# A third size of expert in a mixture-of-experts block: up to 32 rows, in four column groups of TensorE

## The reference

```python
group_p = softmax(h @ group_w + group_b);  g = top_1(group_p)          # 4 groups
e_p = softmax((h @ expert_w + expert_b) inside group g)                # 8 experts in a group
top_p, top_i = top_2(e_p)                                              # 2 experts for a token
y[token] = sum over the two of  g_top * top_p * (silu(x @ w_gate[e]) * (x @ w_up[e])) @ w_down[e]
```

```
layer 0: 71 25 68 92 19 32 20 87 27 20 58 43 37 65 71 63 95 41 51 109 89 26 106 41 23 19 20 16 30 51 7 14
layer 1: 56 27 22 31 53 6 38 55 37 68 81 46 40 71 60 17 15 44 8 25 22 23 26 23 19 15 21 13 16 7 18 21
```

## Time and profile before

| what | value |
|---|---|
| median of three executions | 2321.19 us |
| profiled execution, its span | 2321.44 us, 2319.8 us |
| PE, weight loads of PE, DVE, ACT, POOL busy | 81%, 42%, 31%, 19%, 12% of the span |
| HBM read, written | 529.47 MB, 41.78 MB |
| expert weights loaded | 3 x 64 DMAs of 2048 KB |
| stores of expert rows | 51 of 256 KB, 13 of 512 KB |

### The profile page before, as it was taken

One profiled execution on the slowest core, in us unless ns is written; L12 is line 12 of the kernel. 1 busy time (PEld: TensorE's weight loads), 2 busy tenths in 40 slices (PEclk: granted clock), 3 DMA queues, 4 the chain that ended last, 5 costly groups with the idle time before them and its releaser, 6 DMA issues. The chain is left out here.

```text
span 2319.8 us, 23218 instructions
## 1 busy us (share of the span) xinstructions
PE 1889.0 (81%) x7918; PEld 982.4 (42%) x7919; DVE 716.2 (31%) x1243; ACT 429.8 (19%) x748; POOL 279.3 (12%) x355
## 2 busy tenths in 40 slices
PE   2559999889489999999853899999957989987781
PEld 0125444555334444444412546888533334433330
DVE  1130678553411111111227226555331111111114
ACT  2000233311001111111113114444201111111112
POOL 1020254211110000000014010000011000000001
PEclk9779999989689999999985899999968999998896
DMA  9971119210588999999963102000159999999993
GB/s 369 422 261 43 36 60 248 100 58 28 235 339 342 398 409 412 420 386 371 400 260 142 55 0 82 1 1 1 49 219 357 408 411 402 394 402 395 401 414 132
DMA packets 93246, 572.21 MB, mean 247 GB/s; under 512 B 21016, under 2 KB 35096, under 8 KB 61304
## 3 DMA queue, kind: packets, MB, share of 16 engines
q1 hardware_dynamic: 76864, 515.04, 56.7%
q0 software_dynamic: 8832, 30.68, 3.9%
q10 hardware_dynamic: 7480, 25.57, 2.8%
HBM read 529.47 MB, written 41.78 MB: 246 GB/s over the span
## 5 line engine op out<-in xcount | busy, mean ns | idle before, releaser
L1806 PE MATMUL exp_gps<-moew_wg,all_hT 128*64 128x512 f32 (+1 forms) x1024 | 486.1, 615 | 36.8 <-DMA moew_wu<-in_moe_w_up 34.7
L1807 PE MATMUL exp_ups<-moew_wu,all_hT 128*64 128x512 f32 (+1 forms) x1024 | 484.4, 613 | 0.0
L1806 PEld LDWEIGHTS exp_gps<-moew_wg,all_hT 128*64 128x64 f32 (+1 forms) x1024 | 153.4, 153 | 325.9 <-issue 321.0
L1822 PE MATMUL exp_yps<-moew_wd,all_hT 128*64 128x512 f32 (+1 forms) x512 | 243.7, 607 | 39.5 <-issue 39.5
L1824 PE MATMUL exp_yps<-moew_wd,all_hT 128*64 128x512 f32 (+1 forms) x512 | 244.2, 608 | 0.0
L1916 DVE TENSOR_TENSOR all_hT<-all_hT,exp_ups 64x512 f32<-64x512 f32 (+1 forms) x64 | 44.2, 691 | 586.4 <-ACT all_hT L1867 586.4
L1807 PEld LDWEIGHTS exp_ups<-moew_wu,all_hT 128*64 128x64 f32 (+1 forms) x1024 | 154.2, 153 | 50.9 <-issue 50.9
L577 PE MATMUL abp_ps<-abp_w,all_hT 128*128 128x512 f32 x384 | 166.8, 593 | 0.9 <-PE abp_ps L577 0.6
L1925 DVE COPY exp_y<-exp_yps 64x512 f32<-64x512 f32 (+1 forms) x64 | 44.3, 692 | 298.4 <-PE exp_yps L1824 298.4
L1822 PEld LDWEIGHTS exp_yps<-moew_wd,all_hT 128*64 128x64 f32 (+1 forms) x512 | 71.5, 149 | 147.9 <-issue 147.9
L1867 ACT ACTIVATE all_hT<-exp_gps 64x512 f32<-64x512 f32 (+1 forms) x64 | 37.8, 591 | 485.4 <-PE exp_ups L1807 485.4
(11 more groups left out here) (368 smaller groups left out, 2264.3 us busy)
## 6 DMA issues: line engine op xcount, KB each, us to landing
moew_wg<-in_moe_w_gate SPq DMA_DIRECT2D x64, 2048.0 KB, 23.1
moew_wu<-in_moe_w_up SPq DMA_DIRECT2D x64, 2048.0 KB, 29.0
moew_wd<-in_moe_w_down SPq DMA_DIRECT2D x64, 2048.0 KB, 27.7
ada_w<-in_ada_w SPq DMA_DIRECT2D x12, 4096.0 KB, 25.6
ys<-exp_y ACTq DMA_DIRECT2D x51, 256.0 KB, 8.3
abp_w<-in_ab_w_in SPq DMA_DIRECT2D x6, 2048.0 KB, 8.2
ys<-abp_zero SPq DMA_DIRECT2D x32, 256.0 KB
ys<-exp_y ACTq DMA_DIRECT2D x13, 512.0 KB, 10.1
```

The costliest lines, as they stand in the source:

```text
L1806: nc.tensor.matmul(gps[0:rows, :], x[:, k, 0:rows], w.g[q][:, k, :], start=(k == 0), stop=(k == KD - 1))
L1807: last = nc.tensor.matmul(ups[at:at + rows, :], x[:, k, 0:rows], w.u[q][:, k, :], start=(k == 0), stop=(k == KD - 1))
L1822: nc.tensor.matmul(yps[0][0:rows, :], hT[:, k, 0:rows], w.d[q][:, k, 0:512], start=(k == 0), stop=(k == HT_N - 1))
```

## The change

A third path, Q = 32, is added beside 128 and 64, on all engines.

- PE computes gate and up of a small expert in four column groups: the left and right halves (256 columns) of the gate matrix on PSUM partitions 0 to 31 and 32 to 63, those of the up matrix on 64 to 95 and 96 to 127. So the hidden rows come out as 64 partitions of 256 values, and two transposes take the place of four. The down product has four groups of 256 columns too.
- For that split of the hidden dimension all sizes now take the down matrix in pairs of rows: partition p holds rows 2p, 2p+1 and 256+2p, 256+2p+1, in place of 4p to 4p+3. A partition's 16 KB come from two places of 8 KB each.
- ACT and DVE work on 256 columns for such an expert; each copies its half of the output in two pieces of 32 x 256.
- 32 rows are gathered and 32 stored for it. The zero fill covers rows 32 to 127.

```diff
-                lo = 0 if b >= E else P // 2
+                lo = 0 if b >= E else P // 4
...
 def load_down(sp, a, layer, w, e, q):
-    src = a["moe_w_down"][layer].rearrange("e (p k) n -> e p (k n)", p=P)[bass.ds(e, 1)]
-    sp.dma_start(w.d[q][:].rearrange("p k n -> p (k n)"), src.rearrange("o p m -> (o p) m")).then_inc(w.d_ready[q], 16)
+    src = a["moe_w_down"][layer].rearrange("e (k p two) n -> e p k (two n)", p=P, two=2)[bass.ds(e, 1)]
+    sp.dma_start(w.d[q][:].rearrange("p (k two) n -> p k (two n)", two=2),
+                 src.rearrange("o p k n -> (o p) k n")).then_inc(w.d_ready[q], 16)
...
+        def sized(eng, rows, work):
             with eng.If(rows > H):
                 work(P)
             with eng.Else():
-                work(H)
+                with eng.If(rows > Q):
+                    work(H)
+                with eng.Else():
+                    work(Q)
...
                 def up(rows):
+                    if rows == Q:
+                        for k in range(KD):
+                            for bank, wt, lo in ((gps, w.g[q], 0), (ups, w.u[q], H)):
+                                for j in range(2):
+                                    last = nc.tensor.matmul(bank[lo + j * Q:lo + (j + 1) * Q, 0:HC], x[:, k, 0:Q],
+                                                            wt[:, k, j * HC:(j + 1) * HC],
+                                                            start=(k == 0), stop=(k == KD - 1))
+                        last.then_inc(gu_used, 1)
+                        return
...
                 def down(rows):
+                    if rows == Q:
+                        for k in range(2):
+                            last = nc.tensor.transpose(hps[:, k, 0:H], h_by[H:P, 0, k, :], c.ident[H:P, H:P])
...
+                    if rows == Q:
+                        for k in range(HT_N):
+                            for j in range(4):
+                                last = nc.tensor.matmul(yps[j // 2][j * Q:(j + 1) * Q, 0:HC], hT[:, k, 0:Q],
+                                                        w.d[q][:, k, j * HC:(j + 1) * HC],
+                                                        start=(k == 0), stop=(k == HT_N - 1))
+                        last.then_inc(d_used, 1)
+                        return
```

More of the change, by code:

```diff
@@ L1699, in experts @@
         LOOPS = (E - 1) // S
-        H = P // 2
+        H, Q = P // 2, P // 4
+        HC = HID // 2
         idx = [s.sb(f"idx{i}", [P, 1], I32) for i in range(S)]
@@ L1711, in experts @@
         x_by = [x.rearrange("r (p k) -> r k p", k=KD) for x in xg]
-        h_by = h.rearrange("r (p k) -> r k p", k=HT_N)
+        h_by = h.rearrange("r (k p two) -> r k two p", p=P, two=2)
         xps = [s.ps(f"xps{i}", [P, 4, P]) for i in range(2)]
@@ L1736, in by_rows @@
             rows = eng.value_load(r.cnt[0:1, bass.ds(n, 1)], min_val=0, max_val=TOK)
+            sized(eng, rows, work)
+        def sized(eng, rows, work):
             with eng.If(rows > H):
@@ L1812, in down @@
                     at = 0 if rows == P else H
-                    for k in range(HT_N):
-                        last = nc.tensor.transpose(hps[:, k, 0:rows], h_by[at:at + rows, k, :],
-                                                   c.ident[at:at + rows, at:at + rows])
+                    if rows == Q:
+                        for k in range(2):
+                            last = nc.tensor.transpose(hps[:, k, 0:H], h_by[H:P, 0, k, :], c.ident[H:P, H:P])
+                    else:
+                        for k in range(HT_N):
+                            last = nc.tensor.transpose(hps[:, k, 0:rows], h_by[at:at + rows, k // 2, k % 2, :],
+                                                       c.ident[at:at + rows, at:at + rows])
                     last.then_inc(htr, 1)
@@ L1828, in turn @@
                 rows = pe.value_load(r.cnt[0:1, bass.ds(n, 1)], min_val=0, max_val=TOK)
[L1829 to L1832, removed]
+                sized(pe, rows, up)
                 if more:
@@ L1836, in turn @@
                 pe.wait_ge(ht_done, n + 1)
[L1837 to L1840, removed]
+                sized(pe, rows, down)
             x_transposes(0, 0, 0)
@@ L1866, in silu @@
                     act.wait_ge(h_done, n + 1)
+                    if rows == Q:
+                        nc.scalar.activation(sg[H:P, 0:HC], gps[0:H, 0:HC], ACT.Silu).then_inc(sg_done, 1)
+                        return
                     nc.scalar.activation(sg[at:at + rows, :], gps[0:rows, :], ACT.Silu).then_inc(sg_done, 1)
@@ L1871, in rows_out @@
                     act.wait_ge(y_free[q], i * 16 + 16)
-                    nc.scalar.copy(y[q][0:rows, 0:512], yps[0][0:rows, :]).then_inc(y_act, 1)
+                    if rows == Q:
+                        nc.scalar.copy(y[q][0:Q, 0:HC], yps[0][0:Q, 0:HC])
+                        nc.scalar.copy(y[q][0:Q, HC:2 * HC], yps[0][Q:2 * Q, 0:HC]).then_inc(y_act, 1)
+                    else:
+                        nc.scalar.copy(y[q][0:rows, 0:512], yps[0][0:rows, :]).then_inc(y_act, 1)
                     act.wait_ge(y_act, n + 2)
@@ L1875, in rows_out @@
                     act.dma_start(ys[bass.ds(n, 1), 0:rows].rearrange("o p n -> (o p) n"), y[q][0:rows, :]).then_inc(y_free[q], 16)
[L1877 to L1880, removed]
+                sized(act, rows, silu)
                 if more:
                     x_copy(n + 1, (q + 1) % S)
[L1883 to L1886, removed]
+                sized(act, rows, rows_out)
             x_copy(0, 0)
@@ L1915, in hidden @@
                     dve.wait_ge(sg_done, n + 1)
+                    if rows == Q:
+                        nc.vector.tensor_tensor(h[H:P, 0:HC], sg[H:P, 0:HC], ups[H:P, 0:HC], ALU.mult).then_inc(h_done, 1)
+                        return
                     nc.vector.tensor_tensor(h[at:at + rows, :], sg[at:at + rows, :], ups[at:at + rows, :],
@@ L1921, in rows_out @@
                     dve.wait_ge(htr, n + 1)
-                    nc.vector.tensor_copy(hT[:, :, 0:rows], hps[:, :, 0:rows]).then_inc(ht_done, 1)
+                    if rows == Q:
+                        nc.vector.tensor_copy(hT.rearrange("p (a b) r -> p b a r", b=2)[:, :, :, 0:Q],
+                                              hps[:, 0:2, 0:H].rearrange("p b (a r) -> p b a r", a=2)).then_inc(ht_done, 1)
+                    else:
+                        nc.vector.tensor_copy(hT[:, :, 0:rows], hps[:, :, 0:rows]).then_inc(ht_done, 1)
                     dve.wait_ge(d_used, n + 1)
                     dve.wait_ge(y_free[q], i * 16 + 16)
+                    if rows == Q:
+                        nc.vector.tensor_copy(y[q][0:Q, 2 * HC:3 * HC], yps[1][H:H + Q, 0:HC])
+                        nc.vector.tensor_copy(y[q][0:Q, 3 * HC:4 * HC], yps[1][H + Q:P, 0:HC]).then_inc(y_dve, 1)
+                        return
                     nc.vector.tensor_copy(y[q][0:rows, 512:1024], yps[1][at:at + rows, :]).then_inc(y_dve, 1)
[L1927 to L1930, removed]
+                sized(dve, rows, hidden)
                 if more:
                     x_copy(n + 1, (q + 1) % S)
[L1933 to L1936, removed]
+                sized(dve, rows, rows_out)
             x_copy(0, 0)
```

## The result

Four executions of the changed kernel took 2261.4 to 2274.2 us, median 2267.23 us. The kernel before, beside it on the same chip, took 2320.82 us. The ratio is 0.977 (95% interval 0.974 to 0.979): 2.3% faster. The forecast was 2271.3 us.

What follows compares the result with a forecast made beforehand. DMA bounds layer 1, DMA and PE within 3% layer 0; traffic, idle time and ends less down-matrix cost save 24.0 and 26.1 us, together 50.1 from 2321.4: 2271.3 us. Own range 2250 to 2295 us, 8 in 10 2248 to 2303.

Steps and rivals of the forecast that it cites:

- PE: Small experts' matmuls: four column groups run side by side, step 0.215 us for 0.43, turn 8.6 us for 13.76.
- Rival A: Small experts' matmuls: four groups bring PE nothing, layer 0 keeps its end, 2299 us; chance 0.07.
- Traffic of a small expert: Gather and store of 32 rows: 1.18 us saved an expert (0.62 to 1.73), gather loss taken by row.
- Rival B: Expert DMA: small gather loses as much as a 64-row one, 8 KB pieces cost as 4 KB; 2303 us, chance 0.11.
- What counts is traffic: Expert layers: faster PE alone is worth nothing in layer 1, at most DMA's idle 2% in layer 0.
- Idle DMA in layer 0: Layer 0 expert stretch: of 11 us idle DMA, 5 us gained (0 to 11) as gaps behind small experts close.
- Ends: Last small expert behind each layer's last weights: 3.5 us saved a layer (1 to 7), depending on PE's clock.
- Down matrix: Down weight loads in 8 KB pieces: 1 us cost a layer, bounds 0 and 7.3 us.
- Zero fill: Projection block: 4.2 MB more zeros, some 17 us, hidden by PE; cost 0, at worst about 5 us.
- Rival C: Expert loop: PE's longer loop must refetch instructions, up to 27 us a round, about 2640 us; chance 0.05.
- q8 packets inside the expert loops: Sign in the profile after: instruction-queue packets there would show PE's loop being fetched anew and the forecast wrong.
- What would show it: Profile signs: PE waits for layer 0 weights from about its fifth expert, expert stretches about 518 and 493 us.

Runs made afterwards that it cites:

- PE alone: Changed kernel with small experts gathering and storing 64 rows and the old zero fill, against the kernel before: 2304.5 us, ratio 0.992.
- traffic alone: Kernel before with 32 rows gathered and stored for small experts and the larger zero fill, computing still on 64 rows: 2297.2 us, ratio 0.989.
- the second trace: Changed kernel, unaltered, profiled once more in a later comparison with the kernel before: profiled execution 2259.6 us, median 2265.7 us, ratio 0.976.

## Why the prediction was right, point by point

- **PE.** The step was taken as 0.215 us, measured 0.22. The turn was forecast at 8.6 us, measured 8.25. Rival A is refuted. Behind an idle stretch it can start at half clock, as in the earlier trace rows. The last small expert of layer 0, kernel after (start us, duration us):

```profile
1159.23 0.64 PE L1818 MATMUL exp_gps<-moew_wg,all_hT 128*32 128x256 f32 x2 [6.15 <-DMA moew_wu<-in_moe_w_up]
...
1159.66 0.64 PE L1818 MATMUL exp_gps<-moew_wg,all_hT 128*32 128x256 f32 x2
...
1164.65 0.38 PE L1818 MATMUL exp_gps<-moew_wg,all_hT 128*32 128x256 f32 x2
...
1164.87 0.38 PE L1818 MATMUL exp_gps<-moew_wg,all_hT 128*32 128x256 f32 x2
```

  Behind 6.15 us of idle time the granted clock is 0.50 (1159.2 to 1164.2 us) and steps are 0.43 us apart, as forecast; from 1164.7 us it is 1.00 and they are 0.22 us apart.
- **Traffic of a small expert.** 1.18 us forecast for each. DMA work fell by 16 and 22 us: 1.1 us for each of 14 and 20. The 32-row gather was taken at 0.87 us, in the middle of 0.31 and 1.42. With the forecast's own 1.23 and 1.73 us for the larger gathers the runs bracket it: 0.49 under a 128-row one (1.23 - 0.49 = 0.74), 0.75 under a 64-row one (1.73 - 0.75 = 0.98). A 64-row gather was taken to cost 0.5 us more than a 128-row one, measured as (551.8 - 538.2) / 29 = 0.47. That is near a loss by row (0.87) and far from bytes alone (0.31) and from a fixed loss for each gather (1.42). Rival B is refuted in both its halves, by these runs and by the down matrix alone. Stretches with a 32-row gather, kernel after (last column GB/s), against the earlier trace rows:

```profile
1934.50:1936.90 2.40, 2.40 (x6) 1.12 (x7) 0.69 (x1) 0.58 (x1) 0.00 (x0) 1.00 1.02 335
...
2004.90:2006.70 1.80, 0.00 (x0) 0.00 (x0) 0.63 (x1) 0.49 (x1) 0.00 (x0) 1.00 1.02 314
...
2101.00:2103.00 2.00, 0.00 (x0) 0.00 (x0) 0.00 (x0) 1.28 (x1) 0.00 (x0) 1.00 1.02 303
```

  About half as long as the 4.8 us of a 64-row one, at the same lower rate: sixteen such stretches read 283 to 359 GB/s. This is what the Trainium skill's "SBUF — State Buffer", Door 1: The DMA port swizzle, leads one to expect, that 0 to 31 and 0 to 63 reach the same half of the ports; the traces agree in the rate and in 128 rows going without loss. They do not show the ports themselves, and no run gathered 64 rows into other partitions, so the number of partitions and their place are not told apart.
- **What counts is traffic.** Half right. In layer 1 it is all that counts: 19.8 us from traffic, 3.2 from PE. In layer 0 the sentence that a faster PE alone is worth "at most the idle 2% of DMA" gave 11 us with the ends aside, and PE alone brought 15.4, of which the end is some 3, while traffic alone brought 2.9 of the 13 by which the DMA work fell. There traffic counts only once PE is faster. The sum came out right because both were changed at once.
- **Idle DMA in layer 0.** 5 us forecast. DMA's idle time there went from 29 to 21 us (17 in the second trace); without the layer's end (11 us, then 8 and 5, next point) 18 to 13 and 12 us: 5 to 7.
- **Ends.** From the last weight packet to the last matmul it was 11.0 and 10.8 us before, 7.9 and 8.0 after, 5.4 and 4.8 in the second trace. Saved 3 and 6 us a layer; 3.5 was forecast between 1 and 7. Which of the two comes is a matter of the clock, and by luck the two traces show one each. The last down product of layer 0 in the first and in the second trace of the kernel after (busy us, mean ns):

```profile
L1846 PE MATMUL exp_yps<-moew_wd,all_hT 128*32 128x256 f32 x32 | 3.6, 628 | 0.4 <-issue 0.4
```

```profile
L1846 PE MATMUL exp_yps<-moew_wd,all_hT 128*32 128x256 f32 x32 | 1.9, 381 | 0.4 <-issue 0.4
```

  Same code, at a granted clock of 0.53 (1167.9 to 1171.5 us) and of 1.00 (1161.6 to 1163.5 us in the second trace). This is some of the scatter of the kernel after, and the range had 5 us either way for the ends.
- **Down matrix.** 1 us a layer, measured none.
- **Zero fill.** Forecast to be hidden, which held: the projection block ended at 437.2 us against 436.4. Its size was off. The stores started 0.8 us later and ended at about 412 us, against 408: some 4 us longer, not 17. The 17 were worked out at the rate of stores from 64 partitions, and stores from 96 ran faster (last section). SP's waits at the block's end, kernel after, against the earlier trace rows:

```profile
SPq L72 <- PEq L72: 24.1, 1, 24.1
SPq L72 <- DMA ys<-abp_zero: 5.6, 1, 5.6
```

- **Rival C.** Refuted as a cost of every round. Queues that carried packets from 710 to 1145 us, kernel after:

```profile
q1 hardware_dynamic: 14302, 160.24, 90.4%
q10 hardware_dynamic: 2384, 8.00, 4.6%
q0 software_dynamic: 2128, 7.08, 4.5%
```

  No instruction queue, with 1260 matmul and load instructions in a round. But the prediction had named q8 packets inside the expert loops as a sign of this rival, and there are some: 9 from 1700 to 2272 us, where the kernel before has 5, most of them in the layer's first round and at its end. PE in the gate/up products of the first two small experts of layer 1, kernel after:

```profile
1743.06 0.40 PE L1818 MATMUL exp_gps<-moew_wg,all_hT 128*32 128x256 f32 x1
1745.70 0.41 PE L1818 MATMUL exp_gps<-moew_wg,all_hT 128*32 128x256 f32 x2 [2.24 <-issue]
...
1759.57 0.64 PE L1818 MATMUL exp_gps<-moew_wg,all_hT 128*32 128x256 f32 x2 [3.39 <-issue]
```

  Both gaps lie between two steps of one product, which have nothing to wait for, and a q8 packet lies near the start of each (1743.2 and 1756.9 us; the gaps start at 1743.5 and 1756.2). The second trace has the same two gaps, 2.5 and 3.1 us, with a packet at each. So most likely the new path was fetched there at its first use, and PE stood still for 2 to 3 us, less than the 4.5 us that the rival took. It happens once and not in each round, and in a layer that DMA bounds, where no cost in time is seen. In layer 0 the loop runs without such packets from 710 to 1145 us. The Trainium skill's "Runtime: NRT & Kernel Launch", Instruction fetch mechanics, says that a branch beyond two blocks stalls for a fetch; these 435 us disagree, for a loop nearly twice as long as the one before. The same section's room for 2048 instructions on PE agrees so far as 1260 go. What a loop beyond that does, no run here tried.
- **What would show it.** Besides the q8 packets two signs came otherwise. PE was to wait for weights in layer 0 from about the fifth expert on; it waits 13.4 us between 780 and 860 us, then not at all to 1000 us (experts 10 to 20 all have more than 32 rows), then 22.8 us. And the stretches of the earlier trace rows, less what the layers saved in the first trace, are 539 - 24.8 = 514 and 516 - 24.4 = 492 us in place of 518 and 493.

The errors are small: the sum saved 4 us too little (6 by the second comparison). The down matrix was taken too dear by 1 us a layer, and the ends and the idle time a little low; against them stands the traffic, 38 us of DMA work where 40 were forecast, so part of the closeness is errors that cancel.

## What to carry to other kernels

Before costing a smaller transfer by its bytes, read what all DMA moves while it runs: here 64 rows cost more than 128, and the way to save was to go far below, to 32. Where two bounds lie within 3%, a change to either alone shows little, and parts tested one by one do not add up to the whole (18 + 25 against 54 to 58 us here). A free stretch of DMA ahead of a small transfer that everyone waits for is not free: filling it with weights cost 8 us.

## What the runs showed of the hardware that was not expected

- Stores of 1 KB pieces to `ys` ran faster when they came from partitions 32 to 127 than from 64 to 127. GB/s in 40 slices of 350 to 408 us, kernel before, then kernel after:

```profile
GB/s 378 304 200 199 201 204 200 202 203 188 192 195 194 194 195 200 196 196 196 197 198 196 194 196 194 195 194 195 262 370 362 356 350 345 342 345 341 345 347 212
```

```profile
GB/s 321 386 353 304 309 311 319 270 249 247 234 289 296 274 299 275 266 303 292 283 307 285 293 293 280 269 245 246 266 262 269 315 349 349 345 345 339 340 339 340
```

  About 196 GB/s from 64 partitions, 234 to 319 from 96, 339 to 370 from 128 (the last part of each; the first slices are still weight loads). Half the partitions get little more than half the rate.
- A gather into 64 partitions slows the transfers beside it, one into 128 does not: 0.47 us more a gather with half the bytes, and 26 us more for the same weights over 29 gathers.
- Four column groups of float32 matmuls with 256 columns run fully side by side at either clock, each with its own weight load: 0.22 and 0.43 us a step of four.
- Down matrices in pieces of 8 KB and of 16 KB to a partition cost the same (ratio 1.000 over the whole kernel).
- A loop of 1260 matmul and load instructions a round ran 435 us without a packet of an instruction queue; at first use of a path PE stood 2 to 3 us beside such a packet.
